# Chunk stage of a decoder block: B, K and V turned by transposes, tokens in one half for both heads, and w_down's last unit counted

## The reference

```
h = rms_norm(x);  proj = h @ w_in
y_a = rwkv7_time_mix(proj[:, :RW_COLS])          # 8 heads of 64
y_b = dilated_mixture_attention(proj[:, RW_COLS:])
x += (sigmoid(..) * (y_a @ w_branch_a) + sigmoid(..) * (y_b @ w_branch_b)) @ w_out
x += conv_glu_ffn(rms_norm(x))                   # w_up, conv, gelu, w_down
x += sigmoid(rms_norm(x) @ w_ple_gate) * (p @ w_ple)
out = rms_norm(x)
```

```
Sa = S @ a_t;  S = S * w_t + Sa b_t^T + v_t k_t^T;  y_t = S @ r_t
```

## Time and profile before

| | us |
|---|---|
| median of three runs | 1000.52 |
| the profiled execution, its own time | 1002.22 |
| its span, first to last instruction | 1000.2 |
| TensorE busy | 963.9 (96%) |
| VectorE busy | 395.4 (40%) |
| ScalarE busy | 425.6 (43%) |
| GpSimd busy | 374.6 (37%) |
| 16 DMA engines, main queue | 28.9% |

### The profile page before, as it was taken

One profiled execution on the slowest core, in us unless ns is written; L12 is line 12 of the kernel. 1 busy time (PEld: TensorE's weight loads), 2 busy tenths in 40 slices (PEclk: granted clock), 3 DMA queues, 4 the chain that ended last, 5 costly groups with the idle time before them and its releaser, 6 DMA issues.

```text
span 1000.2 us, 15861 instructions
## 1 busy us (share of the span) xinstructions
PE 963.9 (96%) x6791; PEld 798.4 (80%) x6791; DVE 395.4 (40%) x624; ACT 425.6 (43%) x665; POOL 374.6 (37%) x175
## 2 busy tenths in 40 slices
PE   6999999989999988999999999999999999999796
PEld 4885877777879988888788888888888888888685
DVE  4110258777564435137534434434344400100525
ACT  6244354345564235342345344444434412322556
POOL 2442443332124112334612444444444444444250
PEclk9999999999999989999999999999999999999899
DMA  8431433322111000222722233333333333233032
GB/s 255 105 103 43 106 85 84 85 85 65 43 46 43 5 3 3 64 83 87 232 62 64 84 106 91 100 101 89 106 89 101 100 111 106 85 106 106 28 119 85
DMA packets 115066, 86.45 MB, mean 86 GB/s; under 512 B 2820, under 2 KB 99990, under 8 KB 114998
## 3 DMA queue, kind: packets, MB, share of 16 engines
q1 hardware_dynamic: 114808, 85.37, 28.9%
q10 hardware_dynamic: 190, 0.08, 0.0%
HBM read 83.34 MB, written 2.10 MB: 85 GB/s over the span
## 4 chain that ended last, share of the span: by engine, by line
PE 73%; ACT 2%; DVE 2%; issue 1%; POOL 1%; DVEq 0%; ACTq 0%
PE bank L516 12%; PE bank L518 12%; PE bank L517 12%; PE bank L560 7%; PE bank L562 7%; PE bank L561 7%; PE bank L785 2%; PE bank L795 2%; PE bank L694 1%; PE bank L709 1%; PE bank L682 1%; PE bank L767 1%; PE bank L756 1%; PE bank L735 1%; PE bank L586 1%
## 5 line engine op out<-in xcount | busy, mean ns | idle before, releaser
L496 POOL TENSOR_TENSOR w_lo<-raw,w_hi 128x1024 fp32r<-128x1024 f32 x138 | 333.4, 2416 | 527.5 <-ACT w_hi L1030 527.3
L1030 ACT ACTIVATE w_hi<-raw 128x1024 fp32r<-128x1024 f32 x138 | 146.4, 1061 | 366.1 <-issue 208.8
L516 PE MATMUL bank<-hT_hi,w_hi 128*128 128x512 f32 (+1 forms) x736 | 286.7, 390 | 2.0 <-POOL w_lo L496 1.9
L518 PE MATMUL bank<-hT_hi,w_lo 128*128 128x512 f32 (+1 forms) x736 | 283.2, 385 | 0.0
L517 PE MATMUL bank<-hT_lo,w_hi 128*128 128x512 f32 (+1 forms) x736 | 283.0, 385 | 0.0
L516 PEld LDWEIGHTS bank<-hT_hi,w_hi 128*128 128x128 f32 x736 | 138.3, 188 | 31.2 <-issue 2.1
L518 PEld LDWEIGHTS bank<-hT_hi,w_lo 128*128 128x128 f32 x736 | 138.3, 188 | 27.8
L517 PEld LDWEIGHTS bank<-hT_lo,w_hi 128*128 128x128 f32 x736 | 138.4, 188 | 27.5 <-issue 0.7
L1804 DVE SCALAR_TENSOR_TENSOR cbuf<-bank,params,cbuf 128x511 f32<-128x511 f32 x48 | 36.0, 750 | 133.9 <-ACT cbuf L1367 133.9
L560 PE MATMUL bank<-w_hi,g_hi 128*128 128x512 f32 x184 | 71.7, 389 | 0.0
L562 PE MATMUL bank<-w_hi,g_lo 128*128 128x512 f32 x184 | 71.6, 389 | 0.0
(11 more groups left out here) (258 smaller groups left out, 1303.8 us busy)
## 6 DMA issues: line engine op xcount, KB each, us to landing
raw<-in_w_up_dram SPq DMA_DIRECT2D x48, 512.0 KB, 3.8
raw<-in_w_in_dram SPq DMA_DIRECT2D x33, 512.0 KB, 4.0
raw<-in_w_down_dram SPq DMA_DIRECT2D x24, 512.0 KB, 3.7
raw<-in_w_gate_dram SPq DMA_DIRECT2D x16, 512.0 KB, 3.9
raw<-in_w_out_dram SPq DMA_DIRECT2D x8, 512.0 KB, 4.3
raw<-in_w_ple_gate_dram SPq DMA_DIRECT2D x8, 512.0 KB, 4.5
xs<-in_x_dram SPq DMA_DIRECT2D x4, 512.0 KB, 5.3
raw<-in_w_branch_a_dram SPq DMA_DIRECT2D x4, 512.0 KB, 3.4
```

Of the source, the lines that this page charges most:

```text
L496: nc.gpsimd.tensor_tensor(low(n)[:, :], raw[:, n % RAW_SLOTS, :], high(n)[:, :].bitcast(F32), ALU.subtract).then_inc(*step("pool", ("lo", n)))
L516: nc.tensor.matmul(o, wh, ah, start=first, stop=False)
L518: return nc.tensor.matmul(o, wl, ah, start=False, stop=last)
L1030: nc.scalar.activation(high(u)[:, :], raw[:, u % RAW_SLOTS, :], ACT.Copy) \
```

## The change

`Kb` has b first and k second for both heads, in two full-height products a pair. Tokens of B and U lie in the upper half of the partitions and those of K and V in the lower half for both heads. GpSimd multiplies keys and b by the decay itself (`Kd`, two products a group) in place of the diagonal matrix DG, and B, K and V are turned by TensorE's transposes with the identity. A transpose gives 128 partitions, so V is read through `Vw`, a window that begins 64 words before V, of whose result the lower half is used; the results of V's and u2's products take two banks where they took one. GpSimd's order has `decayed_keys(2)` before `masked(4)` and `decayed_keys(3)` before `masked(5)`. On ScalarE `decays(p)` stands behind the root of unit 3p+2. `ahead` leaves out only the units of w_out and w_ple_gate with slots of their own, so w_down's last unit is counted.

```
@@ ahead
-    shared = [u for u in range(n + 1, len(UNITS)) if SLOT[u] in range(W_SLOTS)]
-    return shared[W_SLOTS - 1] if len(shared) >= W_SLOTS else len(UNITS) - 1
+    rest = [u for u in range(n + 1, len(UNITS)) if not (UNITS[u][0][0] in ("out", "pleg") and UNITS[u][0][1:] > (1, 0))]
+    return rest[W_SLOTS - 1] if len(rest) >= W_SLOTS else len(UNITS) - 1
@@ GpSimd
-            def decay_diagonals(g):
+            def decayed_keys(g):
...
-                nc.gpsimd.tensor_tensor(DG[:, :, :, :], stacked("ident64").unsqueeze(1).unsqueeze(1).broadcast_to([P, 2, NPAIR, CH]),
-                    e.unsqueeze(3).broadcast_to([P, 2, NPAIR, CH]), ALU.mult).then_inc(*step("pool", ("DG", g)))
+                for s in range(2):
+                    nc.gpsimd.tensor_tensor(Kd[:, s, :, :], Kb[:, :, 2 * g + s, :, :].rearrange("p h two t -> p h (two t)"),
+                        e[:, s, :].unsqueeze(2).broadcast_to([P, NPAIR, 2 * CH]), ALU.mult).then_inc(*step("pool", ("Kd", g)))
...
-                nc.gpsimd.tensor_tensor(k, k, stacked("strict_st").unsqueeze(1).broadcast_to([P, NPAIR, CH]), ALU.mult) \
-                    .then_inc(*step("pool"))
+                gp.wait_ge(*previous("pool"))
+                nc.gpsimd.tensor_tensor(k, k, mask8("strict_st")[half(1)], ALU.mult).then_inc(*step("pool"))
+                gp.wait_ge(*previous("pool"))
@@ TensorE
-            def tokens_of_keys(g):
-                pe.wait_ge(*done("pool", "DG", g))
-                o = [begin("BK", g, q) for q in range(2)]
+            def turned(g, label, columns):
+                o = [begin(label, g, q) for q in range(2)]
...
-                            mm = nc.tensor.matmul(o[q][:, n * CH:(n + 1) * CH], keys_and_b(p, q, 2 * g + s),
-                                                  DG[half(q), s, p, :], start=True, stop=True)
-                mm.then_inc(*step("pe", ("BK", g)))
+                            mm = nc.tensor.transpose(o[q][:, n * CH:(n + 1) * CH], columns(s, p, q), stacked("ident64")[half(q)])
+                mm.then_inc(*step("pe", (label, g)))
+            def tokens_of_keys(g):
+                pe.wait_ge(*done("pool", "Kd", g))
+                turned(g, "BK", lambda s, p, q: Kd[half(q), s, p, :])
             def tokens_of_values(g):
-                o = begin("Vt", g)
-                head_products(o, lambda s, p, q: Vv[half(q), p, chunk_cols(2 * g + s)],
-                              lambda s, p, q: stacked("ident64")[half(q)], shift=1).then_inc(*step("pe", ("Vt", g)))
+                turned(g, "Vt", lambda s, p, q: Vw[half(q), up_to(p, 2 * g + s)])
@@ own_values, solved_u
-                        mm = nc.tensor.matmul(o[half(q), p * CH:(p + 1) * CH], KA[half(1 - q), c % 4, p, :],
-                                              v[half(1 - q), c % 2, q, p, :], start=p == 0, stop=c == 0,
+                        mm = nc.tensor.matmul(o[half(q), p * CH:(p + 1) * CH], KA[half(1), c % 4, q, p, :],
+                                              v[half(1), c % 2, q, p, :], start=p == 0, stop=c == 0,
...
-                o = begin("u2", c)
+                o = [begin("u2", c, q) for q in range(2)]
...
-                        mm = nc.tensor.matmul(o[half(q), p * CH:(p + 1) * CH], Xs[half(q), c // 2, c % 2, p, :],
+                        mm = nc.tensor.matmul(o[q][half(0), p * CH:(p + 1) * CH], Xs[half(q), c // 2, c % 2, p, :],
@@ ScalarE
-                if i % 3 == 1:
-                    decays(i // 3)
                 if i % 3 == 2:
...
+                    decays(p)
@@ VectorE
-                for h in range(2):
-                    for t, slot in ((a, h), (k, 1 - h)):
-                        V.tensor_tensor(Kb[half(h), p, :, slot, :], t[half(h)].rearrange("p (c t) -> p c t", t=CH),
-                            Ei[half(h), q, :].rearrange("p (c t) -> p c t", t=CH), ALU.mult).then_inc(*step("dve"))
+                for slot, t in enumerate((a, k)):
+                    V.tensor_tensor(Kb[:, p, :, slot, :], t.rearrange("p (c t) -> p c t", t=CH),
+                        Ei[:, q, :].rearrange("p (c t) -> p c t", t=CH), ALU.mult).then_inc(*step("dve"))
```

More of the change, by code:

```diff
@@ L484, in _ @@
                     identities(1)
-                    decay_diagonals(0)
+                    decayed_keys(0)
                     identities(2)
@@ L489, in _ @@
                     masked(1)
[L490 to L494, removed]
+                    decayed_keys(1)
+                    masked(2)
+                    masked(3)
+                    decayed_keys(2)
+                    masked(4)
+                    decayed_keys(3)
+                    masked(5)
+                    masked(6)
+                    masked(7)
                 gp.wait_ge(*done("act", "hi", n))
@@ L734, in head_products @@
                             n = NPAIR * s + p
-                            mm = nc.tensor.matmul(o[half(q ^ shift), n * CH:(n + 1) * CH], lhs(s, p, q), rhs(s, p, q),
+                            mm = nc.tensor.matmul(o[half(q), n * CH:(n + 1) * CH], lhs(s, p, q), rhs(s, p, q),
                                                   start=True, stop=True)
@@ L744, in product_a @@
                 head_products(o, lambda s, p, q: KK[half(q), p, chunk_cols(2 * g + s)],
-                              lambda s, p, q: Kb[half(q), p, 2 * g + s, q, :]).then_inc(*step("pe", ("A", g)))
+                              lambda s, p, q: Kb[half(q), p, 2 * g + s, 0, :]).then_inc(*step("pe", ("A", g)))
             def keys_and_b(p, q, c):
@@ L1235, in with_r_and_a @@
                         .then_inc(*step("act"))
-                    nc.scalar.activation(KA[half(1 - q), c % 4, :, :].rearrange("p h t -> p (h t)"), o[half(1 - q), 256:512],
+                    nc.scalar.activation(KA[half(1), c % 4, q, :, :].rearrange("p h t -> p (h t)"), o[half(1), 256:512],
                                          ACT.Copy).then_inc(*frees("act", ("RA", c, q), ("DK", c, q)))
@@ L1264, in rec_u @@
                 for q in range(2):
-                    nc.scalar.activation(VU[c // 2 % 2][half(q), c % 2, q, :, :].rearrange("p h t -> p (h t)"),
-                                         psum(("u2", c))[half(q), 0:256], ACT.Copy).then_inc(*frees("act", ("u2", c), ("U", c)))
+                    nc.scalar.activation(VU[c // 2 % 2][half(0), c % 2, q, :, :].rearrange("p h t -> p (h t)"),
+                                         psum(("u2", c, q))[half(0), 0:256], ACT.Copy).then_inc(*frees("act", ("u2", c, q), ("U", c)))
             for g in range(4):
```

26 lines of the change are left out of this document (15 added, 11 removed).

## The result

The changed kernel takes 985.05 us (984.11 to 985.82, 4 runs); the kernel before, timed beside it, 1001.28 us (999.34 to 1003.3, 4 runs). The ratio is 0.9837, with a 95% interval of 0.9823 to 0.985. The profiled execution took 985.69 us with a span of 983.5; before, 1002.22 and 1000.2. So the span lost 16.7 us where I had summed 13.5.

A forecast was written before the change was run, and what follows sets the result against it. TensorE, busy 96% of the time, was taken to bound the kernel, so only its waits or work count. Terms -2.2 - 0.7 - 2.7 - 7.9 = -13.5 us took the 1000.52 median to 987.0, range 983.5 to 993.7.

The forecast's parts named there:

- The likeliest case: Whole kernel: all four parts gain, 987.0 us, own range 984.5 to 991; chance 0.70.
- without any wait for a bank: Recurrence: TensorE waits for no bank; it set the fast end of the range, 983.5 us.
- a chunk 2 that waits as before: Recurrence: chunk 2 keeps its wait, not due to DG alone; price 5.1 us, 992; chance 0.08.
- part 3: Recurrence: GpSimd's new order ends chunk 2's wait and slow clock, new bank waits cost some back; -2.7 us.
- Part 1: Qk units: `decays` behind the root removes two TensorE waits for `w_lo`; -2.2 us, bounds -2.2 and 0.
- the shorter `Kb` is off the path: Qk units: VectorE's two full-height products instead of four half-height ones gain nothing, as TensorE doesn't wait for them.
- `preC` has long been there at the new place: Qk units: `preC` came at 185.4, before unit 11's root near 189, so ScalarE would not wait.
- Part 2: Start of the chunk stage: transposes make keys (0) 0.84 us shorter, 0.1 given back for values (0); -0.7 us.
- that rival: Transposes: the two halves don't run side by side; price 6.6 us, 993.6; chance 0.10.
- The four new waits: Recurrence, chunks 0, 2, 4 and 5: TensorE waits 1.2 to 1.6 us for ScalarE's copies to free banks.
- Part 4: End of w_down: wait for `xn_c` -6.9, faster transposes -2.1, new wait before second ple unit +1.1; -7.9 us.
- The slower rival, the clock: Recurrence, chunks 0 to 5: the clock falls and stays down, up to +30 us and 1017; chance 0.05.

The follow-up runs named there:

- experiment 3: The changed kernel with the exponentials (`decays`) back at their old place, unit 3p+1: 984.94 us, ratio 0.9844.
- experiment 10: The changed kernel with `Kb` written by four half-height products a pair, the exponentials staying at the new place: 985.28 us, ratio 0.9846.
- experiment 6: The changed kernel with the keys turned by a matmul with the identity instead of a transpose, values still transposed: 991.90 us, ratio 0.9905.
- experiment 4: The kernel before with only the diagonals DG of groups 2 and 3 ahead of the masks of chunks 4 and 5 on GpSimd: 997.21 us, ratio 0.9961.
- experiment 5: The changed kernel with GpSimd's old order, `decayed_keys(2)` behind `masked(4)` and `decayed_keys(3)` behind `masked(5)`: 991.08 us, ratio 0.9897.
- experiment 8: The kernel of experiment 7, with a lone unit taking each bank only when it needs it: 980.51 us, ratio 0.9792.
- experiment 1: The changed kernel with the old rule for the slots (`ahead`), undoing the end of w_down: 993.85 us, ratio 0.9938.
- experiment 2: The kernel before with only the new rule of the rounding (`ahead`): 992.50 us, ratio 0.9922.
- experiment 7: The changed kernel with all additional work of the recurrence between `own_values` and `state_and_output`, and `decayed_keys(3)` behind `masked(5)` on GpSimd: 981.52 us, ratio 0.9803.
- experiment 9: The changed kernel with `Kb` in four half-height products a pair and the exponentials at their old place: 987.85 us, ratio 0.987.

## Why the prediction was right, and where its sum was off

The forecast was 987.0 us with a range of 983.5 to 993.7; 985.05 was measured, and the forecast "faster", at 0.89, came true. The likeliest case came true: all four parts gave their gain. The sum was 3.2 us short of the profile's 16.7, and the terms that were too small can be named. The medians hide part of that: I started from 1000.52, while the kernel before took 1001.28 beside the changed one, so the gain is 16.2 where I had 13.5, and the time is off by only 2.0. Two bounds don't follow from their own terms: without any wait for a bank my sum gives 982.7, not the 983.5 of the range, and a chunk 2 that waits as before makes part 3 +2.4, not +1.

**Part 1: the terms right, the size 0.65 short, and two sentences wrong.** The waits for `w_lo` went and nothing came in their place. But I priced them by the idle time that the timeline shows, 0.99 + 1.25. That is counted from the modelled end of a matmul of 0.39 us, while the next one in a full stream starts after 0.227. From start to start the first wait took 1.381 us, 1.15 more than a normal step, and the matmul behind it 0.306 instead of 0.227; the second took 1.633 and 0.340. That makes 1.23 + 1.52 = 2.75 of the 2.85 gained. The wrong sentence is that the shorter `Kb` is off the path: it stood on the path by which those two waits came, `preC` to ScalarE to the rounding to `w_lo`, and alone would have taken them away (experiment 3). The move that I gave the whole gain to is worth it too, but only where the other is missing (experiment 10). The other wrong sentence is that `preC` has long been there at the new place: I set the root near 189, and it came at 184.54. In the changed kernel `preC` ends at 182.6, ahead of the exponentials at 185.15, but with `Kb` as before ScalarE would have stood 0.87 and 1.29 us there (experiment 10).

**Part 2: the sum right, both terms off.** I said -0.84 for the keys and +0.1 for the values, with 1.16 us a group. A group takes 0.64, so keys (0) gave 1.29. Values (0) now take 0.64 as well; keys and values together took 2.37 before (this follows from the first product of `level_xw`, 12.55 us behind `product_a` before and 11.46 now), so the values had taken 0.44 and lost 0.2. Of the 1.09 that is left, 0.35 was given back by u1 (0); what did it, I haven't found. These are the rows of before:

```profile
306.74 3.95 PE L735 MATMUL bank<-Kb,RA 64*64 64x64 f32 x128
...
319.29 3.90 PE L795 MATMUL bank<-Wp,XT 64*64 64x32 f32 x128
```

That 0.74 came out beside my 0.7 is luck: keys 0.45 better, values 0.1 worse and 0.35 given back make up for each other. Experiment 6 says the same from the other side: with the keys as matmuls and the values as transposes it is 147.48 us from the last head sums to u1 (0), before it was 147.45, so the values' transposes give nothing there and the keys' all. The halves do run side by side, as I had chosen, so that rival was wrong. The mistake was the row: I took the price from L756 and from the attention's transposes, whose moving side has 128 columns, while these transposes move an identity of 64.

**Part 3: the mechanism right, the term mis-sized: -4.9 where I had -2.7.** Chunk 2 gave 5.92 (5.1 forecast); chunks 0, 4 and 5 lost 0.06, 1.16 and 0.16 (0.25, 1.6 and 0.6). That is 1.9 of the 2.3 that I was short; the other 0.4 came in chunks 3, 6 and 7, for which I had no term. The four new waits are where I put them and for the copies I named, but 0.75 to 1.04 us long, not 1.2 to 1.6. Six groups of transposes stand in these four chunks, and my sum had five of them on the path, at 0.9 to 1.0 us each. To the next start they took 0.65 (three) and 0.81 (two, in chunks 4 and 5: 376.78 to 377.59 and 383.25 to 384.06). That is about 1.3 of the 1.9; for the rest the groups of chunks 2, 4 and 5 started earlier than I had reckoned. Experiment 4 shows that chunk 2's gain comes from the order on GpSimd, experiment 5 that the change would lose it without that order, and experiment 8 that what the chunks still paid for was the order of the additional work, with its waits for banks. The quarters of the array that u1 and u2 now share cost nothing: L822 and L850 take 0.68 for 16 as before.

**Part 4: right.** -8.1 against -7.9: 7.32 at the wait (I had 6.9: 0.3 of the idle time held back for a late `xn_c`, which was not needed, and about 0.15 for the start-to-start time as in part 1), 2.07 at the transposes, -1.25 at the second ple unit. VectorE's small L1461 took 1.02 us beside GpSimd's `w_lo`, less than the 1.71 of the earlier trace rows. Experiments 1 and 2 give this part alone, from both sides.

**The slower rival, the clock.** The granted clock was 1.00 from 306 to 395 us, through four pairs of wait and transposes. By the rule of the Trainium skill that a transpose is no activity for the clock (TensorE: Matmul & The Clock Gate, Part 4: PE-mode transpose) it might have fallen there; the trace doesn't bear that out, though these pairs are short: a wait of at most 1.04 us and 0.7 us of transposes. A longer one stands at the end of w_down: 32 transposes in 3.66 us and then the wait of 1.01, with no other product in between, and the clock stayed up, here and at the same place in the profiles of experiments 2, 3, 5, 6, 7, 9 and 10.

```profile
921.00:928.00 7.00, 5.99 (x44) 5.31 (x43) 4.64 (x8) 6.06 (x12) 0.00 (x0) 1.00 0.23 74
```

With no product at all it did fall: in the kernel before at 368.6, within the wait of 2.40 us, and in experiment 5 at 365.0, within the wait of 4.08. So the traces speak against that rule for these transposes. But the 3.4 us in experiment 7 began at 353.2, behind a wait of 0.63 us which experiment 8 has at the same place without a fall, so a short fall can come or stay away with the same instructions. What decides that stays open. The two slower runs of experiment 6 had a lower mean clock, but where it fell in them no trace shows.

**The median.** Part of the 16 us between the medians is the clock too: the changed kernel's low stretches are gone but for the last 2 us, and its mean is 0.999 (0.997 to 0.999 over its runs); the kernel before had 6.8 us at the lower level from 368.6, as much from 935.2, and its last 3.5 us, with means of 0.990 to 0.993 over its runs.

## What to carry to other kernels

Price a wait by the start-to-start time on the waiting engine, less its usual step; the idle time shown starts at a modelled end and was short by 0.15 to 0.3 us each here. Before an edit is called off the path, follow who waits for its engine two steps on: here a product on VectorE held up a rounding on ScalarE, a subtraction on GpSimd and a wait of TensorE. And where work is put between the steps of a recurrence, put all of it where the other engine is working on the recurrence's own copy, and queue a helper engine's products by when they are asked for: in the recurrence here that was worth 4.35 us beyond the change (experiment 8; 3.5 of the medians in experiment 7).

## What the runs showed of the hardware

- A float32 transpose of a half-height 64x128 tile onto an identity of 64 columns is issued each 0.03 us on average with the halves of the partitions side by side (16 starts within 0.49 us at 355.26 of the changed kernel, the next work 0.65 after the first). The same product as a matmul leaves two records, and 16 take 1.93 us to the next work, three times as long (experiment 6).
- A wait of TensorE costs its next matmul too: behind the waits at 171.70 and 191.32 of the kernel before, 0.306 and 0.340 us to the following start instead of 0.227, at full granted clock.
- TensorE's granted clock stayed at 1.00 through 3.66 us of float32 transposes and 1.01 us of waiting behind them (922.0 to 926.7 of the changed kernel, and the same place in seven experiments), and fell within waits of 2.40 and 4.08 us without any product (368.6 of the kernel before, 365.0 of experiment 5).
- How long the clock stayed at its lower level differed between executions: 3.4 us in experiments 2 and 7, 6.8 in the kernel before (twice) and experiment 1, 10.2 in experiments 4 and 5. The same place of the same instructions had different ones: chunk 2 had 6.8 us in the kernel before and 3.4 in experiment 2.
- A half-height product on VectorE costs as much as a full one. `Kb`'s four of 64 partitions take 2.60 us near 181 in the kernel before, its two of 128 partitions 1.28 near 180 in the changed one: 0.65 and 0.64 each.
